# Retention gate applied before the norm's scale, head outputs turned in halves, and one whole-row scatter per expert tile

## The chip, the cores and the metric

The kernel runs on one core of one Trainium2 chip. The metric is device time in microseconds (us) of one execution, lower is better. Engines: PE (TensorE, matmuls and transposes), DVE (VectorE), ACT (ScalarE), POOL (GpSimd) and SP (SyncE, which here only issues DMAs). DMAs issued by SP and ACT go through hardware queues (q1 and q10 in the profile), those issued by POOL through a software queue (q0).

## The reference, cut to what matters

One decoder layer on x of 1024 tokens by 1024 columns, in float32. After a norm and one wide projection, two branches run: sparse attention (8 heads, the top 256 keys of each query) and retention; then a mixture of 16 experts, of which each token uses two. The parts that the change touches:

```python
def group_norm_heads(x, g):                       # x: the retention output of a head, 1024 x 256
    mu = mean(x); var = mean(square(x - mu))
    return (x - mu) * rsqrt(var + EPS) * g
ret = group_norm_heads(retention_chunkwise(...), ret_norm_g)
y_ret = (silu(r_gate) * ret) @ w_ret_branch       # 4 heads of 256 columns

# experts: out[token] += p * expert(token), two experts a token, on top of the residual h
```

## The kernel before, in words

Each engine runs a straight list of instructions, written out by hand; semaphores order the engines. Matmuls are made of three products of a high and a low part (w_hi, w_lo, n_hi, n_lo). Weight chunks of 128x512 come through `w_raw` (SP), are split by ACT (`hi`, line 1512) and POOL (`lo`, line 2644).

**Retention stage.** PE follows `ret_order` (line 646). For head h, `phase1(h)` turns keys and forms scores and chunk states, `phase2(h)` the outputs, `turn(h)` (line 1262) transposes the 8 normed and gated row tiles of `ro` into four banks, named by (j, half). Between them stand four `first_half` products of the attention gates, `first(0)` to `first(3)`. Around this, for a head h: ACT copies the outputs to `ro` (`out_phase2`, line 1697), POOL makes the means (`means`), ACT squares each of the 8 row tiles with the mean as bias (`out_stats`, line 1704), POOL makes 1/sqrt (`scales`, lines 2631 and 2632), DVE scales all tiles by (ro + mean) * rstd and then multiplies by the gate in one 128x2048 instruction (`out_phase2`, lines 2146 and 2149), which sets `o_done`. SP loads the next head's gate after `o_done`, and ACT applies Silu to it (`silu_gate`, line 1668). After PE's turn ACT copies the four banks, with the gains, to `rT_out` and issues the stores to `ret_dram` itself (`out_turn`, lines 1717 and 1720). DVE also copies the gate products to `first_out`, which SP stores (`store_first`). In between DVE searches the top-256 bound of each query row (`pick_top`), a generator of which each call `pick(us)` runs so much; it ends with `dist`, line 2202.

**Start of attention.** STEPS are 64, one for each (query tile t, head h), m = 8t + h. A query tile is loaded by SP to `qrow` (`load_q`), scaled by POOL (`scale_rows`, line 2709), turned by PE in two halves (`turn_q`, line 993; for t >= 2 at steps m = 8(t-1) + 1 and + 4), split by ACT and DVE into `qT_hi` and `qT_lo`. A step is: logits (PE), add of the distances (DVE, 2286), Exp (ACT, 1779), scaling (DVE, 2294), transposes (PE, 1296), copy (ACT, 1800), product with v. `qT_lo(1,1)` and `aT` lie where `rT_out` was, so DVE at (1,1) and ACT at the first `pv` wait for all stores of `ret_dram` (`ret_stored`). POOL issues the copies and accumulating DMAs of weight sums between its query tiles (`copy_sums`, `add_sums`).

**Experts.** 31 tiles of 128 token rows. POOL gathers the rows (`gather_rows`, line 2816), PE does gate, up and down, ACT scales the result by the token's weight into one of three `e_y` buffers (`rows_out`, line 1977), and POOL adds it to the output by indirect DMA (`add_rows`, line 2806): two scatters of half rows (2 KB), each of which waits until the scatter of the same half of the tile before has landed. ACT waits for a buffer's scatters of three tiles before. The end of the kernel waits for all.

Of the kernel before, what the change touches and what calls it, by code (L numbers as in the profile page):

```python
# [198 lines left out]
def program(nc, w, scratch, out):  # L199
    ctx = ExitStack()  # L200
    with ctx:
# [34 lines left out]
        nt_at = place[0]  # L236
        n_hi = sb("n_hi", [P, KT, S], F32R)
# [17 lines left out]
        def r1t(name, shape, off, dt=F32):  # L255
# [26 lines left out]
        rT_out = [r1t(f"rT_out{i}", [P, BANK], at) for i, at in enumerate((18688, 17152, 17664, 18176))]  # L282
        first_out = [sb(f"first_out{i}", [P, BANK], at=at) for i, at in enumerate(
            (up_at, cst_at + 4 * K_TRI, cst_at + 4 * K_REL, cst_at + 4 * (K_REL + BANK)))]
# [17 lines left out]
        qT_lo_first = [r1t(f"qT_lo_first{g}", [P, 4, P], 4096 + 3 * g * S + BANK, F32R) for g in range(2)]  # L302
# [89 lines left out]
        o_mu, o_var, o_rstd, o_done = sem("o_mu"), sem("o_var"), sem("o_rstd"), sem("o_done")  # L392
# [25 lines left out]
        ey_full, ey_read, ey_out = sem("ey_full"), sem("ey_read"), [[sem(f"ey_out{i}{j}") for j in range(2)] for i in range(3)]  # L418
# [233 lines left out]

        SQ_ACT = range(NT - 1)
# [78 lines left out]
        def _(sp):  # L732
# [113 lines left out]
            load_q(1)  # L846
            store_first(3)
# [4 lines left out]
            for i in range(2):  # L852
                sp.wait_ge(first_stored[i], 16 * 8)
# [120 lines left out]
            for i in range(3):  # L974
                for j in range(2):
                    sp.wait_ge(ey_out[i][j], 16 * ((NTILE + 2 - i) // 3))
# [3 lines left out]
        def _(pe):  # L980
# [293 lines left out]
            for m in range(STEPS + LAG + 4):  # L1274
                if m < STEPS:
# [7 lines left out]
                    for k0 in range(0, nk, BANK):  # L1283
                        n = min(BANK, nk - k0)
                        last = three(ps[:, c + k0:c + k0 + n].rearrange("p (t k) -> p t k", k=P),
                                     (qT_hi[t % 2][:, h, :], (qT_lo[t % 2] if t else qT_lo_first)[h // 4][:, h % 4, :]),
# [213 lines left out]
        def _(act):  # L1500
# [200 lines left out]
            def out_stats(h):  # L1701
                act.wait_ge(o_mu, h + 1)
                for c in range(NT):
                    inst = A(junk2[:], ro[h % 2][:, c, :], ACT.Square, bias=small[:, 104 + c:105 + c], accum_out=small[:, 112 + c:113 + c])
                    seq(inst) if c < NT - 1 else inst.then_inc(o_var, 1)
                act.wait_ge(o_var, h + 1)

            def out_turn(h):
                if h == 0:
                    act.wait_ge(proj_last, 64)  # L1710
                for n in range(4):
# [32 lines left out]
            for i in range(4):  # L1744
                c = ga + 4 * i + NH - 1
                if i == 3:
                    out_phase2(3)
                    out_turn(2)
# [10 lines left out]
                if i in (0, 3):  # L1759
                    silu_gate(i)  # L1760
                if i < 3:
                    hi(c + 2)
                    hi(c + 3)
            out_qT(0, 0)
            out_qT(0, 1)
            out_turn(3)
            A(small[:, 497:498], small[:, 500:501], ACT.Exp)

            for m in range(STEPS + LAG + 4):
                if m < STEPS:  # L1770
                    t, h = divmod(m, HA)
                    if m == 7 * HA:
                        for c in range(m6, m6 + NH):
                            hi(c)
                    if m in LATE_AT:
# [5 lines left out]
                if pv_at(m) and pv_at(m)[2] == 3:  # L1781
# [3 lines left out]
                    if t == 0 and g == 0:  # L1785
# [177 lines left out]
            def last_rows_out(i):  # L1963
                n = tile_at(i)
                for j in range(2):
                    act.wait_ge(ey_out[i.buffer][j], 16 * i.third)
# [4 lines left out]
            def rows_out(i):  # L1971
                act.wait_ge(ey_full, i.n + 1)
                if i.reached(3):
                    for j in range(2):
                        act.wait_ge(ey_out[i.buffer][j], 16 * i.third)
# [41 lines left out]
        def _(dve):  # L2017
# [859 lines left out]
```

## Time and profile before

| | |
|---|---|
| three runs | 1491.22, 1497.29, 1498.73 us, median 1497.29 |
| the profiled execution | 1492.21 us, span 1490.1 us, mean granted clock 0.962 |
| busy | PE 1389.7 us (93%), DVE 1115.1, ACT 869.0, POOL 677.2 |
| DMA | 336.76 MB, mean 226 GB/s |

The span runs from the first to the last instruction; about 2.1 us of the execution's time lie outside it. The stages by time in the span: projections until about 485 us, retention until 600, attention 600 to 777, gates, branches and output product until 1150, routing until 1185, experts until the end.

### The profile page before, as it was taken

To read this page: it belongs to the slowest core of one execution; us is meant where nothing else is said; L and a number is where in the kernel's file an instruction comes from. 1 tells how busy PE (TensorE), PEld (TensorE's weight loads), DVE (VectorE), ACT (ScalarE), POOL (GpSimd) and SP (SyncE) were. 2 spreads that over 40 slices of the span, in tenths; PEclk is the share of its full clock that TensorE was granted. 3 is DMA by queue.
4 is the path that set the end of the run, shared out by engine and by line. 5 is a ranking of instruction groups with operands and counts; after the bars stand their busy time and mean duration, and the time that the engine had idled before them with its cause. 6 is when DMAs were issued, how large, how long until landed. Compare 5 with 4: busy or idle time off the path is not lost.

```text
span 1490.1 us, 19630 instructions
## 1 busy us (share of the span) xinstructions
PE 1389.7 (93%) x6518; PEld 1137.7 (76%) x6518; DVE 1115.1 (75%) x1581; ACT 869.0 (58%) x1528; POOL 677.2 (45%) x474
## 2 busy tenths in 40 slices
PE   6999999999999798799999999999997699999995
PEld 6887777788888687667767887887885588888884
DVE  6828999999989954666634447989643699999994
ACT  5237544435773577577744447363345388888884
POOL 3622254445454624121124545555332467665665
PEclk9997999999999999699999999999999699999998
DMA  5997688796765684978958886574346898989995
GB/s 187 360 255 139 161 262 308 205 277 195 259 216 175 207 261 159 258 209 188 250 126 298 225 231 221 197 251 139 111 147 232 300 300 202 311 230 357 282 278 71
DMA packets 153364, 336.76 MB, mean 226 GB/s; under 512 B 14896, under 2 KB 32688, under 8 KB 149040
## 3 DMA queue, kind: packets, MB, share of 16 engines
q1 hardware_dynamic: 111904, 227.49, 44.8%
q0 software_dynamic: 28496, 82.85, 26.1%
q10 hardware_dynamic: 12864, 25.17, 4.5%
q8 instruction: 53, 0.87, 0.2%
q14 instruction: 47, 0.39, 0.1%
HBM read 323.92 MB, written 125.83 MB: 302 GB/s over the span
## 4 chain that ended last, share of the span: by engine, by line
PE 67%; DVE 19%; DMA 4%; ACT 4%; issue 3%; POOL 2%; SPq 0%; ACTq 0%; DVEq 0%; POOLq 0%
PE ps L985 18%; PE ps L987 18%; PE ps L986 18%; DVE hits L2160 4%; PE ps L1306 4%; DVE dist L2123 2%; PE ps L1440 2%; DVE n_lo L2050 2%; PE ps L1296 2%; DMA w_raw<-sums_dram 1%; DMA a_raw<-att_dram 1%; PE ps L1257 1%; DMA ret_dram<-rT_out 1%; DVE ranks L2195 1%; DVE top_change L2177 1%
## 5 line engine op out<-in xcount | busy, mean ns | idle before, releaser
L2644 POOL TENSOR_TENSOR w_lo<-w_raw,w_hi 128x512 fp32r<-128x512 f32 (+1 forms) x264 | 377.4, 1446 | 426.2 <-ACT w_hi L1512 424.0
L1512 ACT CAST w_hi<-w_raw 128x512 fp32r<-128x512 f32 (+1 forms) x264 | 161.0, 617 | 306.4 <-PE ps L987 232.6
L985 PE MATMUL ps<-n_hi,w_hi 128*128 128x512 f32 x624 | 246.0, 394 | 13.6 <-POOL w_lo L2644 9.7
L987 PE MATMUL ps<-n_hi,w_lo 128*128 128x512 f32 x624 | 243.9, 391 | 0.0
L986 PE MATMUL ps<-n_lo,w_hi 128*128 128x512 f32 x624 | 243.8, 391 | 0.0
L2582 DVE TENSOR_TENSOR e_lo<-e_raw,e_hi 128x2048 fp32r<-128x2048 f32 x93 | 213.3, 2295 | 21.9 <-ACT e_hi L1956 21.9
L985 PE MATMUL ps<-w_hi,n_hi 128*128 128x512 f32 (+1 forms) x528 | 204.7, 388 | 8.9 <-POOL w_lo L2644 4.2
L986 PE MATMUL ps<-w_lo,n_hi 128*128 128x512 f32 (+1 forms) x528 | 203.0, 384 | 0.0
L987 PE MATMUL ps<-w_hi,n_lo 128*128 128x512 f32 (+1 forms) x528 | 202.9, 384 | 0.0
L1956 ACT CAST e_hi<-e_raw 128x2048 fp32r<-128x2048 f32 x93 | 177.8, 1914 | 32.5 <-PE ps L987 17.3
L2806 POOL DMA_INDIRECT out<-e_y,dest x62 | 142.9, 2305 | 94.4 <-DMA out<-e_y,dest 66.0
L2160 DVE TENSOR_SCALAR_CACHE_REDUCE hits<-dist,top_bound 128x384 uint8<-128x384 f32 (+2 forms) x192 | 171.9, 940 | 0.4
L985 PEld LDWEIGHTS ps<-n_hi,w_hi 128*128 128x128 f32 x624 | 117.6, 189 | 42.3 <-POOL w_lo L2644 15.7
L987 PEld LDWEIGHTS ps<-n_hi,w_lo 128*128 128x128 f32 x624 | 117.5, 188 | 24.7
L986 PEld LDWEIGHTS ps<-n_lo,w_hi 128*128 128x128 f32 x624 | 117.7, 189 | 24.1 <-issue 0.2
L985 PEld LDWEIGHTS ps<-w_hi,n_hi 128*128 128x128 f32 x528 | 100.9, 191 | 29.6 <-issue 7.1
L987 PEld LDWEIGHTS ps<-w_hi,n_lo 128*128 128x128 f32 x528 | 100.8, 191 | 18.5
L986 PEld LDWEIGHTS ps<-w_lo,n_hi 128*128 128x128 f32 x528 | 101.0, 191 | 17.7
L985 PE MATMUL ps<-e_hi,x_hi 128*128 128x512 f32 x248 | 101.0, 407 | 2.4 <-DVE x_lo L2586 2.4
L987 PE MATMUL ps<-e_hi,x_lo 128*128 128x512 f32 x248 | 97.9, 395 | 0.0
L986 PE MATMUL ps<-e_lo,x_hi 128*128 128x512 f32 x248 | 97.7, 394 | 0.0
L2286 DVE CUSTOM_DVE_ANT_0 prob<-ps,dist 128x128 f32<-128x128 f32 (+7 forms) x64 | 48.4, 756 | 37.9 <-PE ps L987 37.2
(287 smaller groups left out, 2668.3 us busy)
## 6 DMA issues: line engine op xcount, KB each, us to landing
w_raw<-sums_dram SPq DMA_DIRECT2D x128, 256.0 KB, 4.1
e_raw<-in_w_gate SPq DMA_DIRECT2D x64, 512.0 KB
e_raw<-in_w_up SPq DMA_DIRECT2D x64, 512.0 KB
e_raw<-in_w_down SPq DMA_DIRECT2D x32, 1024.0 KB
w_raw<-in_w_in SPq DMA_DIRECT2D x80, 256.0 KB, 4.7
sums_dram<-in_w_in POOLq DMA_DIRECT2D x20, 1024.0 KB, 10.8
sums_dram<-in_w_in SPq DMA_DIRECT2D x16, 1024.0 KB, 11.5
sums_dram<-sums_dram POOLq DMA_DIRECT2D x16, 1024.0 KB, 8.9
```

The lines of the kernel that those rows point to most:

```text
L985: mm(out, a[0], b[0], start=first, stop=False, skip_group_check=skip)
L986: mm(out, a[0], b[1], start=False, stop=False, skip_group_check=skip)
L987: return mm(out, a[1], b[0], start=False, stop=last, skip_group_check=skip)
L1296: last = tr(bank(name)[:, kt % 4 * P:(kt % 4 + 1) * P], prob[h % 4][:, kt * P:(kt + 1) * P], ident)
L1306: last = mm(bank(name), kvu[:, kt, DH:2 * DH], pT[:, kt, g], start=kt == 0, stop=kt == t)
L1512: nc.scalar.copy(w_hi[c % NH][:, :width], split_from(c)[:, :width]).then_inc(hi_ready, 1)
L1956: nc.scalar.copy(split_at(e_hi, i, j)[:], e_raw[i.buffer][j][:]).then_inc(ehi_done[j], 1)
L2160: seq.mark(V.tensor_scalar(hits[i % 2][:, :(t + 1) * P], scores(t), bounds(i), None, op, ALU.add, accum_out=sums[:, i:i + 1]))
L2286: bk.read(V.tensor_tensor_reduce(out=prob[h % 4][:, :nk], in0=ps[:, c:c + nk], in1=dist[:, tile_off(t):tile_off(t) + nk], scale=-(2.0 ** - ...
L2582: V.tensor_tensor(split_at(e_lo, i, j)[:], e_raw[i.buffer][j][:], split_at(e_hi, i, j)[:].bitcast(F32), ALU.subtract).then_inc(elo_done[j], 1)
L2644: G.tensor_tensor(w_lo[c % NH][:, :width], split_from(c)[:, :width], w_hi[c % NH][:, :width].bitcast(F32), ALU.subtract).then_inc(lo_ready, 1)
L2806: G.indirect_dma_start(out=out_halves, out_offset=bass.IndirectOffsetOnAxis(ap=dest[j][:, n:n + 1], axis=0), in_=e_y[i.buffer][:, j * BANK ...
```

## The change

The gate is multiplied in first, by one instruction per row tile, (ro + mean) * gate, each as soon as ACT has squared that tile (`o_sq` in place of `o_var`), and then comes the multiplication by rstd, which counts `o_done` after four and after eight tiles. `o_gated` stands between and is what the next gate's load and the next means wait for. PE's `turn` does the first half of the tiles for both j, then the second. ACT's Silu stands ahead of its squares in all heads. The copies of head 2 go from ACT to DVE and their stores to SP; the Exp table load is moved ahead of `out_qT(0, 0)`. `qT_lo` of the tiles 0 and 1 and `first_out` lie elsewhere, and the waits for `ret_stored` and `first_stored` stand later. The calls of `pick` are spread. The scatter adds whole rows of 4 KB, one per tile.

```diff
-        dest = [sb(f"dest{j}", [P, 32], U32) for j in range(2)]
-        out_halves = out.rearrange("r (j n) -> (r j) n", j=2)
+        dest = sb("dest", [P, 32], U32)
...
+        rT_out.insert(1, sb("rT_out1", [P, BANK], at=up_at))
+        first_out = [sb(f"first_out{i}", [P, BANK], at=n_hi_at + 4 * (i * S + BANK)) for i in range(4)]
...
+        qT_lo_early = [[r1t(f"qT_lo_early{2 * t + g}", [P, 4, P], 4096 + at * S + BANK, F32R) for g, at in enumerate(pair)]
+                       for t, pair in enumerate(((0, 3), (1, 2)))]
...
+        TURN_ORDER = (0, 2, 1, 3)
... sync: load_gate
-                    sp.wait_ge(o_done, h)
+                    sp.wait_ge(o_gated, h)
...
             load_q(1)
+            for n in TURN_ORDER:
+                j, half = divmod(n, 2)
+                bk.wait_read(sp, ("rT", 2, j, half))
+                row = (2 * 2 + j) * P
+                sp.dma_start(ret_dram[row:row + P, half * BANK:(half + 1) * BANK], rT_out[n][:]).then_inc(ret_stored[n % 2], 16)
             store_first(3)
             load_q(2)
...
             sp.wait_ge(dist_done, NT)
-            for i in range(2):
-                sp.wait_ge(first_stored[i], 16 * 8)
             sp.dma_start(cst[:, K_TRI:], w["cst"][:, K_TRI:]).then_inc(rest_in, 16)
... tensor: turn
-                pe.wait_ge(o_done, h + 1)
-                for j in range(2):
-                    for half in range(2):
+                for half in range(2):
+                    pe.wait_ge(o_done, 2 * h + half + 1)
+                    for j in range(2):
... scalar
-                    seq(inst) if c < NT - 1 else inst.then_inc(o_var, 1)
-                act.wait_ge(o_var, h + 1)
+                    inst.then_inc(o_sq, 1)
+                    act.wait_ge(o_sq, NT * h + c + 1)
...
                 if i == 3:
                     out_phase2(3)
-                    out_turn(2)
                 if i in (1, 2):
                     out_phase2(i)
                     out_phase1(i + 1)
                 hi(c)
+                silu_gate(i)
                 out_stats(i)
                 if i in (1, 2):
-                    silu_gate(i)
                     out_turn(i - 1)
                 if i < 3:
                     hi(c + 1)
-                if i in (0, 3):
-                    silu_gate(i)
...
+            A(small[:, 497:498], small[:, 500:501], ACT.Exp)
             out_qT(0, 0)
             out_qT(0, 1)
             out_turn(3)
-            A(small[:, 497:498], small[:, 500:501], ACT.Exp)
...
-                    if t == 0 and g == 0:
+                    if t == 1 and g == 0:
                         for i in range(2):
                             act.wait_ge(ret_stored[i], 32 * HR)
... vector
             def out_phase2(h):
-                dve.wait_ge(o_rstd, h + 1)
-                for c in range(NT):
-                    inst = V.tensor_scalar(ro[h % 2][:, c, :], ro[h % 2][:, c, :], small[:, 104 + c:105 + c], small[:, 120 + c:121 + c], ALU.add, ALU.mult)
-                seq(inst)
-                dve.wait_ge(silu_done, h + 1)
-                V.tensor_tensor(ro[h % 2][:], ro[h % 2][:], gate[:], ALU.mult).then_inc(o_done, 1)
+                dve.wait_ge(silu_done, h + 1)
+                for c in range(NT):
+                    dve.wait_ge(o_sq, NT * h + c + 1)
+                    inst = V.scalar_tensor_tensor(ro[h % 2][:, c, :], ro[h % 2][:, c, :], small[:, 104 + c:105 + c], gate[:, c, :], ALU.add, ALU.mult)
+                inst.then_inc(o_gated, 1)
+                dve.wait_ge(o_gated, h + 1)
+                dve.wait_ge(o_rstd, h + 1)
+                for c in range(NT):
+                    inst = V.tensor_scalar(ro[h % 2][:, c, :], ro[h % 2][:, c, :], small[:, 120 + c:121 + c], None, ALU.mult)
+                    if c % 4 == 3:
+                        inst.then_inc(o_done, 1)
+
+            def out_turn(h):
+                for n in TURN_ORDER:
+                    j, half = divmod(n, 2)
+                    name = ("rT", h, j, half)
+                    dve.wait_ge(ret_stored[n % 2], 32 * h)
+                    bk.wait_full(dve, name)
+                    bk.read(V.tensor_scalar(rT_out[n][:], bank(name), gains[:, GRT + 2 * h + j:GRT + 2 * h + j + 1], None, ALU.mult), name)
...
             pick(8)
             out_phase1(1)
-            pick(1e9)
+            pick(3)
             out_phase2(0)
             keep_first(0)
+            pick(3)
...
-                if (t, g) == (2, 0):
-                    dve.wait_ge(first_stored[0], 16 * 8)
-                if (t, g) == (1, 1):
+                if (t, g) in ((2, 0), (3, 1)):
                     for i in range(2):
                         dve.wait_ge(ret_stored[i], 32 * HR)
...
                 out_phase2(i)
                 keep_first(i)
+                pick(1e9)
+            out_turn(2)
             out_phase2(3)
...
-            for j in range(2):
-                inst = V.tensor_scalar(dest[j][:], row_at, 2.0, float(j), ALU.mult, ALU.add)
-            inst.then_inc(dest_done, 1)
+            V.tensor_copy(dest[:], row_at).then_inc(dest_done, 1)
... gpsimd
-                for j in range(2):
-                    pool.wait_ge(ey_read, i.n + 1 + (j if (i + 1).reached(NTILE) else 0))
-                    if i.reached(1):
-                        pool.wait_ge(ey_out[(i - 1).buffer][j], 16 * ((i - 1).third + 1))
-                    G.indirect_dma_start(out=out_halves, out_offset=bass.IndirectOffsetOnAxis(ap=dest[j][:, n:n + 1], axis=0),
-                                         in_=e_y[i.buffer][:, j * BANK:(j + 1) * BANK], in_offset=None,
-                                         compute_op=ALU.add).then_inc(ey_out[i.buffer][j], 16)
+                pool.wait_ge(ey_read, i.n + 1 + ((i + 1).reached(NTILE)))
+                if i.reached(1):
+                    pool.wait_ge(ey_out[(i - 1).buffer], 16 * ((i - 1).third + 1))
+                G.indirect_dma_start(out=out, out_offset=bass.IndirectOffsetOnAxis(ap=dest[:, n:n + 1], axis=0),
+                                     in_=e_y[i.buffer][:], in_offset=None,
+                                     compute_op=ALU.add).then_inc(ey_out[i.buffer], 16)
```

## Rows read from the trace of the kernel before

**Rows 1.** Windows: us, each engine's busy time (instructions), clock, DMA share, GB/s.
```profile
580.00:600.00 20.00, 13.65 (x67) 11.65 (x65) 10.18 (x15) 11.14 (x27) 7.73 (x8) 0.84 0.49 159
1300.00:1400.00 100.00, 100.00 (x495) 84.52 (x494) 92.95 (x65) 86.78 (x76) 61.26 (x31) 1.00 0.96 294
```
**Rows 2.** Timeline of 505 to 530: start, us, engine, line [idle before <- releaser].
```profile
511.09 1.23 DVE L2202 SCALAR_TENSOR_TENSOR dist<-cst,dist 128x1024 f32<-128x1024 f32 x1
...
512.35 1.23 DVE L2131 TENSOR_TENSOR sT<-sT,cst 128x1024 f32<-128x1024 f32 x1
...
518.16 2.07 PE L1257 MATMUL ps<-rv,sT 128*128 128x256 f32 x4 [5.87 <-DVE state L2137]
```
**Rows 3.** Timeline, the last head from ACT's copies of head 2 to the first Exp.
```profile
577.62 0.68 ACT L1717 ACTIVATE rT_out<-ps,gains 128x512 f32<-128x512 f32 x1
...
582.19 0.62 ACT L1512 CAST w_hi<-w_raw 128x512 fp32r<-128x512 f32 x1 [0.45 <-ACT rT_out L1717]
...
587.79 2.19 ACT L1668 ACTIVATE gate<-gate 128x512 f32<-128x512 f32 x4
...
588.12 1.63 POOL L2632 TENSOR_TENSOR small<-small 128x8 f32<-128x8 f32 x1
...
589.79 4.41 DVE L2146 TENSOR_SCALAR ro<-ro,small 128x256 f32<-128x256 f32 x8 [17.06 <-POOL small L2632]
589.83 1.90 POOL L2709 TENSOR_TENSOR qrow<-qrow,small 128x1024 f32<-128x1024 f32 x1
...
591.67 2.78 POOL L2685 DMA_DIRECT2D sums_dram<-in_w_in  x4
...
596.58 3.68 PE L1269 MATMUL ps<-cst,ro 128*128 128x128 f32 x16 [6.35 <-DVE ro L2149]
...
602.31 1.28 ACT L1767 ACT_TABLE_LOAD   x1 [0.39 <-ACT rT_out L1717]
...
603.71 0.39 ACT L1779 ACTIVATE prob<-prob,small 128x128 f32<-128x128 f32 x1
```
**Rows 4.** Timeline of 586 to 632, what the first steps of attention wait for.
```profile
600.94 0.60 SPq L799 DMA_DIRECT2D qrow<-proj_dram  x1
...
613.91 0.69 DVE L2266 TENSOR_TENSOR qT_lo<-ps,qT_hi 128x512 fp32r<-128x512 f32 x1 [2.45 <-DMA ret_dram<-rT_out]
...
614.83 1.89 POOL L2709 TENSOR_TENSOR qrow<-qrow,small 128x1024 f32<-128x1024 f32 x1 [20.38 <-DMA qrow<-proj_dram]
...
617.12 1.06 PE L993 MATMUL ps<-cst,qrow 128*128 128x128 f32 x4
```
**Rows 5.** DMA queues of 600 to 602: packets, MB, share; then an issue and its landing time.
```profile
q0 software_dynamic: 105, 0.41, 90.2%
...
qrow<-proj_dram SPq DMA_DIRECT2D x1, 512.0 KB, 13.8
```
**Rows 6.** DMA queues of 604 to 606.
```profile
q0 software_dynamic: 104, 0.37, 51.8%
q10 hardware_dynamic: 102, 0.20, 27.4%
```
**Rows 7.** The chain of waits in the experts: start, us, what.
```profile
1358.45 0.90 PE ps L1440 x8
1367.81 0.90 PE ps L1440 x8
```
**Rows 8.** All issues: KB each, median us to landing; then the scatter line's own.
```profile
e_x<-n_dram,token POOLq DMA_INDIRECT x31, 9.5
```
**Rows 9.** The scatters of line 2806, 62 of them, from issue to landing.
```profile
DMA to landing us min/median/max: 4.6/7.3/12.1
```
**Rows 10.** The chain of waits at the end: start, us, what.
```profile
1474.26 4.69 DMA out<-e_y,dest
```
**Rows 11.** POOL's timeline at the end: the first half of tile 29, the last of tile 30.
```profile
1471.11 1.55 POOL L2806 DMA_INDIRECT out<-e_y,dest  x1 [1.06 <-ACT e_y L1977]
...
1479.70 1.55 POOL L2806 DMA_INDIRECT out<-e_y,dest  x1 [1.59 <-DMA out<-e_y,dest]
```

More of the change, by code:

```diff
@@ L236, in program @@
         nt_at = place[0]
+        n_hi_at = place[0]
         n_hi = sb("n_hi", [P, KT, S], F32R)
@@ L281, in program @@
         gate = r1t("gate", [P, NT, DV], 15104)
-        rT_out = [r1t(f"rT_out{i}", [P, BANK], at) for i, at in enumerate((18688, 17152, 17664, 18176))]
-        first_out = [sb(f"first_out{i}", [P, BANK], at=at) for i, at in enumerate(
-            (up_at, cst_at + 4 * K_TRI, cst_at + 4 * K_REL, cst_at + 4 * (K_REL + BANK)))]
+        rT_out = [r1t(f"rT_out{i}", [P, BANK], at) for i, at in ((0, 18688), (2, 17664), (3, 18176))]
+        rT_out.insert(1, sb("rT_out1", [P, BANK], at=up_at))
+        first_out = [sb(f"first_out{i}", [P, BANK], at=n_hi_at + 4 * (i * S + BANK)) for i in range(4)]
         junk2 = r1t("junk2", [P, DV], 7168)
@@ L301, in program, with qT_lo_of @@
              (wr_at + 4 * BANK * (NR + 2 * NH - 1), r1 + 4 * 18432)])]
-        qT_lo_first = [r1t(f"qT_lo_first{g}", [P, 4, P], 4096 + 3 * g * S + BANK, F32R) for g in range(2)]
+        qT_lo_early = [[r1t(f"qT_lo_early{2 * t + g}", [P, 4, P], 4096 + at * S + BANK, F32R) for g, at in enumerate(pair)]
+                       for t, pair in enumerate(((0, 3), (1, 2)))]
+        def qT_lo_of(t, g):
+            return qT_lo_early[t][g] if t < 2 else qT_lo[t % 2][g]
         prob = [r1t(f"prob{i}", [P, S], 4096 + i * S) for i in range(4)]
@@ L417, in program @@
         slot_done = sem("slot_done")
-        ey_full, ey_read, ey_out = sem("ey_full"), sem("ey_read"), [[sem(f"ey_out{i}{j}") for j in range(2)] for i in range(3)]
+        ey_full, ey_read, ey_out = sem("ey_full"), sem("ey_read"), [sem(f"ey_out{i}") for i in range(3)]
         dest_done, p_done2 = sem("dest_done"), sem("p_done2")
@@ L1710, in out_turn @@
                     act.wait_ge(proj_last, 64)
-                for n in range(4):
+                for n in TURN_ORDER:
                     j, half = divmod(n, 2)
@@ L1774, in _ @@
                             hi(c)
+                    if m == LATE_AT[0]:
+                        for i in range(2):
+                            act.wait_ge(first_stored[i], 16 * 8)
                     if m in LATE_AT:
@@ L1964, in last_rows_out @@
                 n = tile_at(i)
+                act.wait_ge(ey_out[i.buffer], 16 * i.third)
                 for j in range(2):
-                    act.wait_ge(ey_out[i.buffer][j], 16 * i.third)
                     act.wait_ge(ey_full, i.n + 1 + j)
@@ L1973, in rows_out @@
                 if i.reached(3):
-                    for j in range(2):
-                        act.wait_ge(ey_out[i.buffer][j], 16 * i.third)
+                    act.wait_ge(ey_out[i.buffer], 16 * i.third)
                 n = tile_at(i)
@@ L2143, in out_phase2 @@
             def out_phase2(h):
+                dve.wait_ge(silu_done, h + 1)
[4 more added lines that the diff above has]
+                dve.wait_ge(o_gated, h + 1)
                 dve.wait_ge(o_rstd, h + 1)
                 for c in range(NT):
[L2146 to L2149 removed]
+                    inst = V.tensor_scalar(ro[h % 2][:, c, :], ro[h % 2][:, c, :], small[:, 120 + c:121 + c], None, ALU.mult)
+                    if c % 4 == 3:
+                        inst.then_inc(o_done, 1)
+            def out_turn(h):
+                for n in TURN_ORDER:
+                    j, half = divmod(n, 2)
[3 more added lines that the diff above has]
+                    bk.read(V.tensor_scalar(rT_out[n][:], bank(name), gains[:, GRT + 2 * h + j:GRT + 2 * h + j + 1], None, ALU.mult), name)
             def scores(t):
@@ L2265, in out_qT @@
                 name = ("qT", t, g)
-                bk.read(V.tensor_tensor((qT_lo[t % 2] if t else qT_lo_first)[g][:].rearrange("p h q -> p (h q)"), bank(name),
+                bk.read(V.tensor_tensor(qT_lo_of(t, g)[:].rearrange("p h q -> p (h q)"), bank(name),
                                         qT_hi[t % 2][:, 4 * g:4 * g + 4, :].rearrange("p h q -> p (h q)").bitcast(F32), ALU.subtract), name)
@@ L2568, in _ @@
             seq(V.scalar_tensor_tensor(row_at, row_at, -1.0, tok_at, ALU.add, ALU.add))
-            for j in range(2):
-                inst = V.tensor_scalar(dest[j][:], row_at, 2.0, float(j), ALU.mult, ALU.add)
-            inst.then_inc(dest_done, 1)
+            V.tensor_copy(dest[:], row_at).then_inc(dest_done, 1)
             def slot_weights():
@@ L2715, in means @@
                 if h:
-                    pool.wait_ge(o_done, h)
+                    pool.wait_ge(o_gated, h)
                 G.tensor_scalar(small[:, 104:112], small[:, 96:104], -1.0 / DV, 0.0, ALU.mult, ALU.add).then_inc(o_mu, 1)
             def scales(h):
-                pool.wait_ge(o_var, h + 1)
+                if h:
+                    pool.wait_ge(o_done, 2 * h)
+                pool.wait_ge(o_sq, NT * (h + 1))
                 rstd(small[:, 120:128], small[:, 112:120], NT, DV, (o_rstd, 1))
@@ L2831, in _ @@
             for i in range(3):
-                for j in range(2):
-                    pool.wait_ge(ey_out[i][j], 16 * ((NTILE + 2 - i) // 3))
+                pool.wait_ge(ey_out[i], 16 * ((NTILE + 2 - i) // 3))
             for j in range(3):
```

8 lines of the change are left out of this document (3 added, 5 removed).

## The prediction

> **What bounds the kernel now.** I read the windows first. PE is the engine of most of the time: in the experts it is busy for 100.00 of 100 us at full clock, DMA at 0.96 beside it, and a tile starts every 1367.81 - 1358.45 = 9.36 us [rows 1, 7]. Nothing that the change does to DVE, ACT or POOL there can pay, except at the very end. At the end of retention it is otherwise: from 580 to 600 PE is busy for 13.65 us of 20 and its clock falls to 0.84 [rows 1]. So the timeline was read from there on. PE stands idle twice in retention: 5.87 us before 518.16, for DVE's states of head 1 [rows 2], and 6.35 us before 596.58, for the gated tiles of head 3 [rows 3]. Then comes a chain that PE only follows: turn of head 3, four copies by ACT, table load, first Exp at 603.71 [rows 3], and in attention's first tiles waits for DMAs: DVE 2.45 us for the last stores of `ret_dram`, POOL 20.38 us for `qrow(2)`, which is scaled just in time for PE's turn at 617.12 [rows 4].
>
> **The pick calls: nothing.** The last instruction of the search (L2202, 511.09) already stands before the states of head 1 (L2131, 512.35) [rows 2]: `pick(8)` ends the search, and `pick(1e9)` behind it finds nothing to do. So the first stall of 5.87 us stays. Here the change does not do what it says. Had it moved work, at most those 5.87 us could be won, which is outside my sum.
>
> **Heads 0 to 2: nothing.** DVE has 8 + 8 small instructions in place of 8 + one large one. The large one ends a semaphore before PE's turn at 596.58, so it takes 596.5 - (589.79 + 4.41) = 2.3 us. Eight small ones cost 2.5 (the 4.41 of a scaling less the 1.90 of POOL's instruction beside it) [rows 3]. PE turns head h only after the outputs of head h + 1, and the next gate is loaded sooner, so all of it is covered. If it were not, it would cost 0.2 us a head and a semaphore, 1 in all.
>
> **Head 3, up to the scale.** ACT loses its four copies of head 2: from 577.62 to 582.19, 4.57 us [rows 3], of which DVE now has 4 copies in a time when it waits (17.06 us idle) [rows 3], and SP four stores, issued before the gate products of `store_first(3)`, which are not there before DVE makes them. In their place Silu, 2.19 us, comes ahead of the squares; the cast of 0.62 was there before too. The squares start at 577.62 + 0.62 + 2.19 = 580.4 and take 587.79 - 582.81 = 5.0, so they end at 585.5 in place of 587.79. That is 2.2 us. POOL's 1/sqrt follows (0.3 + 1.63), and DVE starts to scale at 587.6 in place of 589.79.
>
> **Head 3, behind the scale.** Before: 4.41 + 2.3 and a semaphore, so PE's turn began 6.8 us after the scale began [rows 3]. After: four tiles. They still collide with POOL's 1.90 us multiplication of `qrow(1)`, which stands right behind 1/sqrt in both kernels, so 1.9 + 4 x 0.31 = 3.1 us: first half ready at 590.7, second at 592.0. The other instruction, (ro + mean) * gate, follows each square and is done but for the last tile (0.4 us) when the scale arrives. PE ends its last `first_half` at 590.2 (idle 6.35 before 596.58), so what is late next on PE is PE itself. ACT's copies begin at about 591.3 (before: 602.31 - 0.39 - 4.1 = 597.8). They end at about 595.4; the table load of 1.28 us and its 0.1 of issue lie in ACT's idle time ahead of them. If the load were needed twice, for Exp and for the copies' function, that costs 2.6. First Exp at about 595.9 in place of 603.71: 7.8 us gained at this point.
>
> The Trainium skill has a rule for the collision (page "SBUF — State Buffer", section Who interferes with whom): DVE and GpSimd share a port pair as an exclusive lock, so whichever comes second waits for the whole instruction. The 4.41 us for eight tiles beside POOL's 1.90 us agree. By the rule alone the 1.9 us would stay in the changed kernel, as in my sum; without a collision the first half would be ready 1.9 earlier, but PE would be no earlier than 590.2.
>
> **What is late next.** The wait for the stores of `ret_dram` (2.45 us) goes, since the (1,1) buffer lies elsewhere; at (2,0) the stores have had until about 612 to land. But PE's step 9 needs `qrow(2)`. Its load is issued behind `store_first(3)`: DVE makes those after its `out_qT`, two of 0.69 [rows 4]. The load was issued 4.4 us after DVE's end at 596.5, so now at 592.0 + 4.4 = 596.4 in place of 600.94 [rows 4]. It took 13.8 us to land [rows 5], because POOL's four copies of 1 MB, issued at 591.67 [rows 3], hold the DMA engines: from 600 to 602 q0 alone moved data, at 90.2% of the engines [rows 5], though SP and ACT had issued before; from 604 to 606 q0 has 51.8% and ACT's queue alone 27.4% [rows 6]. POOL issues the copies at 589.6 now, 2.1 earlier. Lower bound: `qrow(2)` keeps its own 13.8: landed at 596.4 + 13.8 = 610.2. Upper: the burst ends as long after the copies as before (600.94 + 13.8 - 591.67 = 23.1): 612.7. The constants' load (364 KB, now not behind the wait for `first_stored`) adds at most 364/512 of a `qrow`, under 1 us, to the same queue, behind `qrow(2)`. I take 611.0, nearer its own time, since stores and load move together as they did before. POOL scales in 1.9 and PE turns 0.3 later, at 613.2 in place of 617.12: 3.9. Meanwhile ACT and DVE have finished steps 8 and 9, which at 617.12 they had not (DVE was put back by 2.45); I put that at 1.3 between 0 and 2.5. **Attention: 5.2 us gained, bounds 2.2 and 7.8** (landed at 612.7 and nothing advanced, and the whole of the head start). Later `qrow` tiles and POOL's accumulating DMAs are issued off PE's and POOL's progress, so they move with it, and the stages behind are PE-bound.
>
> A rule of the Trainium skill speaks to this point (page "DMA: Bandwidth & Descriptors", Queues, rings and completion order, on arbitration): each engine goes round the queue rows that have work, packet by packet. The first two microseconds do not show that (q0 alone); from 604 on the shares come near it. What it would make of the time is rival 2.
>
> **The scatter.** POOL issues 31 in place of 62, and per tile saves one of some 2.3 us, hidden by PE in both kernels. At the end: before, the half scatter issued at 1474.26 landed 4.69 later [rows 10], and the last was issued at 1479.70 [rows 11] and lands by 1484.3; what follows until 1490.1 I leave as it is. After: tile 29's scatter is issued when its first half was, at 1471.1 [rows 11]; tile 30's rows are ready before it has landed, so it waits for it. A whole row is not in the trace. From below it is a half's 4.6 [rows 9], from above a half's end after a second one's issue, 1.55 + 4.69 = 6.2 [rows 10, 11]; gathers of whole rows took 9.5 in the loaded stage where halves took 7.3 [rows 8, 9], a ratio of 1.3, so 5.9. Landing of 29 at 1477.0, issue of 30 at 1477.7 (0.75 from landing to issue, as 1479.70 - 1474.26 - 4.69), landing at 1483.6. **0.7 us gained, bounds +3.3 (4.6 twice) and -1.6 (landing times of 7).** One DVE instruction less for `dest` is off the path.
>
> **Sum.** 1492.2 (the profiled execution: span 1490.1 and 2.1 around it) - 5.2 - 0.7 = 1486.3. That execution was the second lowest of four: with the three runs the middle is 1494.8, and the runs spread over 7.5 us. 1494.8 - 5.9 = 1488.9 is what I give as the time; against the median of 1497.29 about 3 more may be spread.
>
> **Rivals.**
> 1. The burst decides alone: `qrow(2)` lands at 612.7 or later, the advance of ACT and DVE is lost in PE's clock, which stands at half after the longer wait. Gain 2.2 + 0.7: 1491.9. For it: q0 alone in the first microseconds [rows 5]. Against: `qrow(2)` is issued 4.6 earlier. Chance 0.19.
> 2. The hardware queues get their turn at once, or `qrow(2)` is in early: all of 7.8 stays, 8.5 with the tail: 1486.3. For it: the shares from 604 on [rows 6]. Against: 600 to 602 [rows 5]. Chance 0.26.
> 3. Slower: whole-row scatters fall behind PE. Scatter i+1 is issued only when i has landed, so a tile costs its landing plus 0.75. With halves that is 7.3 + 0.75 = 8.05 under 9.36 [rows 7, 9]. With whole rows at the end's difference (5.9 - 4.6) it is 8.6 + 0.75 = 9.35, just PE's pace, and at the gather's 9.5 it is 10.25, 0.9 a tile over PE. Three `e_y` buffers hide 2 x 9.36 = 18.7 us of lag, but the end waits for the lag: 27 tiles x 0.9 = 24, less 8 that the last three tiles win back when the weights are in (9.36 - 6.65 each). So 16 against attention's 5.2: 1494.8 - 5.2 + 16 = 1505.6. It decides from a landing of 8.9 us on. For it: DMA share 0.96 [rows 1], half scatters up to 12.1 [rows 9]. Against: the bytes are the same with half the packets. Chance 0.14.
> 4. The pipeline absorbs the head start by other waits of attention (POOL's chain of accumulating DMAs): 0.7 only: 1494.1. Chance 0.03.
>
> The forecast has 0.38. Likeliest one's own range: 1483 to 1494. The range for 8 in 10 takes in rivals 1, 2 and the spread of the runs, and the mild half of rival 3: 1480 to 1500.
>
> A measurement tells 0.5%, about 7.5 us, from no change. The forecast's 5.9 is under it, with a third of its chance beyond it through the unknown landings: 0.12 faster, 0.26 same. Rival 2 at 8.5: 0.22 faster, 0.04 same. Rivals 1 and 4: same, 0.22. Rival 3: slower but for its mild cases, 0.12, and 0.02 same. Faster 0.34, same 0.54, slower 0.12.
>
> **What the changed profile would show.** PE without the 6.35 before the turn of head 3 and with it at about 590 to 592; the first Exp at about 596; no wait of DVE for `ret_dram`; POOL's scaling of `qrow(2)` at about 611 and PE's turn at 613; the idle of 5.87 before 518 unchanged; tiles of the experts still 9.36 apart; whole-row scatters landing in 8 to 9 us, uncontended in 5.9. I am wrong if the scatters' median is over 8.9, if the table load comes twice, or if PE's turn of step 9 comes outside 610 to 616.

## The result, and the profile after

The changed kernel takes 1512.52 us (1509.13 to 1515.12 over three runs) against 1497.29: a ratio of 1.0086 with a 95% interval from 1.0051 to 1.0121, so it is slower by 0.86%, some 13 us. The forecast was 1488.9, its range 1480 to 1500. The profiled execution took 1509.13, its span is 1506.7.

Both halves of the change show in the trace. First the head start of attention: the timeline of the changed kernel, from POOL's 1/sqrt of the last head to the third query tile, to be set beside [rows 3, 4].

```profile
589.33 1.63 POOL L2649 TENSOR_TENSOR small<-small 128x8 f32<-128x8 f32 x1
591.04 1.90 POOL L2726 TENSOR_TENSOR qrow<-qrow,small 128x1024 f32<-128x1024 f32 x1
591.07 4.19 DVE L2157 TENSOR_SCALAR ro<-ro,small 128x256 f32<-128x256 f32 x8 [1.88 <-POOL small L2649]
592.88 2.63 POOL L2702 DMA_DIRECT2D sums_dram<-in_w_in  x4
594.03 0.66 PE L1276 MATMUL ps<-cst,ro 128*128 128x128 f32 x4 [0.38 <-DVE ro L2157]
...
599.51 0.57 SPq L804 DMA_DIRECT2D qrow<-proj_dram  x1
...
600.05 0.40 ACT L1785 ACTIVATE prob<-prob,small 128x128 f32<-128x128 f32 x1 [0.40 <-ACT rT_out L1724]
...
616.25 1.89 POOL L2726 TENSOR_TENSOR qrow<-qrow,small 128x1024 f32<-128x1024 f32 x1 [20.74 <-DMA qrow<-proj_dram]
...
618.20 1.11 PE L1000 MATMUL ps<-cst,qrow 128*128 128x128 f32 x4 [7.79 <-POOL qrow L2726]
```

PE's idle time of 6.35 us ahead of the turn has shrunk to 0.38, and the first Exp is 3.66 us earlier than in [rows 3] although this execution was 2.46 us late before the edit does anything (L2136's product, the one of 512.35 in [rows 2], starts at 514.81). That is 6.1 us. Then PE waits 7.79 us for `qrow(2)`, and its turn, at 617.12 in [rows 4], is at 618.20. The DMA view of 600 to 602 has the load's issue and its time to land, 13.8 in [rows 5]:

```profile
q0 software_dynamic: 106, 0.39, 58.7%
q10 hardware_dynamic: 105, 0.20, 27.3%
q1 hardware_dynamic: 51, 0.10, 14.4%
...
qrow<-proj_dram SPq DMA_DIRECT2D x1, 512.0 KB, 16.7
```

Three queues share the engines there, where q0 was alone in [rows 5], and still the load takes longer. The Trainium skill (page "DMA: Bandwidth & Descriptors", Queues, rings and completion order) has each engine go round the rows with work packet by packet; this trace is nearer to that than the one before, and it did not bring the load in early, as rival 2 would have it.

Next the experts. The view of the instructions that touch `e_y` in the changed kernel: the scatters, what they wait for, who waits for them, and their landing ([rows 9]).

```profile
L2824 POOL DMA_INDIRECT out<-e_y,dest x31: 1552/1690/3634, 1206.0 to 1494.9; - x31
...
  DMA out<-e_y,dest: 162.5, 29
...
  ACT e_y L1982: 8.5, 3
...
DMA to landing us min/median/max: 5.9/7.9/13.2
```

From the first issue to the last a tile takes (1494.9 - 1206.0) / 30 = 9.63 us, over the 9.36 of [rows 7]. The median landing of 7.9 doesn't explain this; the chain that ended last does, since there the landings stand one after another (start, us, what):

```profile
1389.13 11.85 DMA out<-e_y,dest
1401.02 0.75 issue
1401.77 7.84 DMA out<-e_y,dest
1409.65 0.75 issue
1410.40 10.90 DMA out<-e_y,dest
1421.34 0.75 issue
1422.09 11.01 DMA out<-e_y,dest
1433.14 0.75 issue
1433.90 10.49 DMA out<-e_y,dest
...
1473.62 6.77 DMA out<-e_y,dest
1480.43 0.71 issue
1481.14 6.15 DMA out<-e_y,dest
1487.33 0.71 issue
1488.04 6.11 DMA out<-e_y,dest
```

Four of the first five take 10.5 to 11.9 us, over PE's pace; the last three, when all weights are loaded, take 6.1 to 6.8. The lag passes through the three `e_y` buffers to ACT, and then to PE, which is busy for 100 of 100 us from 1300 to 1400 as in [rows 1] and has its gaps behind 1400 (the windows, columns as there):

```profile
1400.00:1440.00 40.00, 37.21 (x179) 30.38 (x178) 33.80 (x25) 32.30 (x29) 14.79 (x8) 1.00 0.97 329
1440.00:1480.00 40.00, 38.81 (x178) 32.10 (x178) 33.34 (x23) 30.23 (x28) 11.01 (x6) 0.96 0.60 126
1480.00:1506.70 26.70, 3.02 (x12) 2.17 (x12) 0.42 (x1) 1.45 (x3) 4.66 (x3) 0.67 0.39 59
```

On ACT, whose timeline follows, the scaled rows of a tile wait for their buffer three times:

```profile
1421.38 1.12 ACT L1982 ACTIVATE e_y<-ps,small 128x1024 f32<-128x1024 f32 x1 [1.39 <-DMA out<-e_y,dest]
1433.19 1.12 ACT L1982 ACTIVATE e_y<-ps,small 128x1024 f32<-128x1024 f32 x1 [3.83 <-DMA out<-e_y,dest]
1444.47 1.11 ACT L1982 ACTIVATE e_y<-ps,small 128x1024 f32<-128x1024 f32 x1 [3.31 <-DMA out<-e_y,dest]
...
1483.65 0.69 ACT L1974 ACTIVATE e_y<-ps,small 128x512 f32<-128x512 f32 x1 [0.61 <-PE ps L994]
```

The account of the two traces: the last scatter is issued at 1494.90, 15.2 us behind the 1479.70 of [rows 11]. The first rows are gathered at 1173.91 instead of 1170.16, which is 3.75 of it. ACT's last `e_y` starts at 1483.65 where it started at 1474.58, so another 5.3 was lost between, where the waits of ACT shown above (8.5 us in all) stand. The rest, 6.15, is the queue of scatters at the end: from that last `e_y` to the last issue 11.25 us pass in place of 5.1.

### The profile page after: what moved, and what is told of

The parts are those of the page before. It is cut to its first block, busy times and chain, and to the rows that moved or that the text cites. A ratio compares the mean times of both kernels' runs of the same rounds, so it can differ in the third digit from the quotient of the medians.

```text
span 1506.7 us, 19601 instructions
## 1 busy us (share of the span) xinstructions
PE 1391.5 (92%) x6518; PEld 1134.5 (75%) x6518; DVE 1119.1 (74%) x1612; ACT 865.3 (57%) x1524; POOL 597.1 (40%) x443
## 4 chain that ended last, share of the span: by engine, by line
PE 48%; DVE 23%; DMA 15%; issue 5%; ACT 5%; POOL 3%; SPq 1%; ACTq 0%; DVEq 0%; POOLq 0%
PE ps L992 13%; PE ps L994 12%; PE ps L993 12%; DVE hits L2178 7%; DMA out<-e_y,dest 7%; PE ps L1313 4%; DVE n_lo L2055 2%; DVE dist L2128 2%; PE ps L1303 2%; DMA sums_dram<-in_w_in 2%; DMA t_raw<-turned_dram 2%; PE ps L1447 1%; POOL w_lo L2661 1%; DMA qrow<-proj_dram 1%; DVE top_change L2195 1%
## 5 line engine op out<-in xcount | busy, mean ns | idle before, releaser
L992 PE MATMUL ps<-n_hi,w_hi 128*128 128x512 f32 x624 | 246.6, 395 | 12.3 <-POOL w_lo L2661 10.4
L992 PEld LDWEIGHTS ps<-n_hi,w_hi 128*128 128x128 f32 x624 | 117.9, 189 | 41.4 <-POOL w_lo L2661 14.6
L2824 POOL DMA_INDIRECT out<-e_y,dest x31 | 64.3, 2073 | 183.1 <-DMA out<-e_y,dest 153.9
```

Source lines behind the costliest of these rows:

```text
L992: mm(out, a[0], b[0], start=first, stop=False, skip_group_check=skip)
L2824: G.indirect_dma_start(out=out, out_offset=bass.IndirectOffsetOnAxis(ap=dest[:, n:n + 1], axis=0), in_=e_y[i.buffer][:], in_offset=None, c ...
```

## Experiments

All kernels here were timed against the kernel before in five rounds, in three groups, each group with the kernel before on one and the same chip; its medians there are 1498.2, 1498.8 and 1498.3. Ratios are to it, and kernels of different groups are compared by their ratios.

**Taking the change apart.** The first kernel has the scatter part of the diff alone, the second the retention part alone.

> The kernel before with the scatter of whole rows alone; nothing of the retention heads is changed. Theory A (the whole-row scatters are the loss: each waits for the landing of the one before it, and one landing with its issue lasts longer than the two half rows' landings lasted side by side): the last scatter is issued about 11 us later than in the kernel before, and the time is 9 to 12 us longer, about 1507. Theory B (the retention edit is the loss, and what the experts lose is carried over from it): within 2 us of the kernel before. Under A the PE is below 95% busy from the start of the last fifteen tiles on, and the scatters' median gap is over 9.4 us.

> The changed kernel with the two scatters of half rows back; the retention edit is all that is left of the change. Theory A (the whole rows are the loss): the time is that of the kernel before within 4 us, on either side; what the trace of the changed kernel shows ahead of the experts (3.7 us later from the first to the last store of attention) is partly run to run. Theory B (the retention edit is the loss): 8 us or more longer. My recorded forecast for this part by itself was 5.2 us shorter; the load of the third query tile landing 16.7 us after its issue instead of 13.8 should bring that to 1 to 2 us shorter.

Whole rows alone: 1509.94, ratio 1.0076 [1.0054, 1.0098]. Retention edit alone: 1496.24, ratio 0.9986 [0.9972, 1.0000], about 2 us gained. So the loss is the scatter's, 11 to 12 us, and theory B falls. In the trace with whole rows alone the last scatter is issued at 1494.2, 14.5 us behind the 1479.70 of [rows 11], of which 4.0 had passed before the first gather (1174.17). Two signs set for theory A did not come: PE is 96% busy from 1343 to 1482, not below 95%, and the median step from one scatter's issue to the next is 8.8 us, not over 9.4. It is the mean that is over PE's pace, (1494.2 - 1206.4) / 30 = 9.59 us; why the two differ is told below.

**What in the whole rows costs.** The third kernel keeps them, but lets them overlap; the fourth keeps the halves and adds a dependency.

```diff
-                if i.reached(1):
-                    pool.wait_ge(ey_out[(i - 1).buffer], 16 * ((i - 1).third + 1))
-                G.indirect_dma_start(out=out, ...
+                if i.reached(2):
+                    pool.wait_ge(ey_out[(i - 2).buffer], 16 * ((i - 2).third + 1))
+                G.indirect_dma_start(out=scratch["spare"] if i.n % 2 else out, ...
```

> As the kernel before with whole-row scatters, but the scatters of odd tiles add their rows to a scratch tensor instead of the output (so half of the experts' contribution is left out of the output), and each scatter waits for the landing of the one two tiles before it. Bytes, rows and instructions are the same. If the chain of landings is what costs (theory A), the loss is gone: within 2 us of the kernel before or 1 to 5 us shorter, and PE over 97% busy in the experts. If whole rows cost by their bytes in the queue or by the time that GpSimd spends on issuing them, the time stays at that of the whole rows alone, 9 to 12 us longer than before.

```diff
                     if i.reached(1):
-                        pool.wait_ge(ey_out[(i - 1).buffer][j], 16 * ((i - 1).third + 1))
+                        for k in range(2):
+                            pool.wait_ge(ey_out[(i - 1).buffer][k], 16 * ((i - 1).third + 1))
```

> The kernel before, two scatters of half rows to a tile, but each of them waits for the landing of both halves of the tile before. The same bytes and descriptors as before, one more dependency. If the loss comes from one chain that includes the last byte of a tile (theory A), part of it shows here: 3 to 10 us longer than the kernel before. If it comes from the whole row's own landing (rows of 4 KB against 2 KB), the kernel is within 2 us of before.

Two destinations: 1497.86, ratio 0.9989 [0.9972, 1.0007]. The loss is gone, with the same rows, bytes and instructions. This kernel changes two things at once, the destination and the wait, but it was not that the landings got shorter: those to `out` have a median of 10.2 us, those to the scratch tensor 7.1, all together 10.1 where whole rows alone have 7.5. Halves that wait for both halves: 1542.48, ratio 1.0291 [1.0266, 1.0316], 44 us and far over the 3 to 10 expected. There the first half of a tile waits for the second of the last one, which is issued later than the first, so a tile costs that delay, a landing and the next issue: (1537.0 - 1212.0) / 30 = 10.8 us from the first scatter to the last. ACT waited 42.7 us for `e_y` in that trace. It is the chain that costs, and two chains side by side are what the two halves were good for.

**Why the chain is too slow.** A pair of kernels without the traffic of the weights:

```diff
-                G.tensor_scalar(fresh[:, 1:31], small[:, 465:495], 0.0, 1.0, ALU.max, ALU.min)
+                G.tensor_scalar(fresh[:, 1:31], small[:, 465:495], 0.0, 0.0, ALU.max, ALU.min)
```

> The kernel before with whole-row scatters, and the loads of the experts' weights are switched off from the fourth tile on (all tiles after the third compute with weights that are there already, so the experts' contribution is not the reference's). Theory A2 (a whole row's landing fits the pace of a tile, 9.36 us, when it has the queues for itself, 5.8 us and 0.7 to the next issue, and exceeds it only beside a new expert's 3 MB of weights, 10 to 12.3 us): the loss of 12 us against the same with half rows shrinks to 0 to 3 us, landings have a median under 6.5 us and PE keeps its pace to the last tile. Rival (the whole row in one chain is slower in itself): it stays over 8 us slower than the half rows with the same loads switched off.

> The kernel before, half-row scatters, with the loads of the experts' weights switched off from the fourth tile on, as the pair of the kernel above. All theories: within 2 us of the kernel before, since PE is at its pace of 9.36 us a tile there already; the median landing of the half rows falls from 7.3 us to about 5.

Whole rows: 1498.96, ratio 1.0007 [0.9986, 1.0027]. Halves: 1498.45, ratio 0.9999 [0.9981, 1.0017]. The loss of whole rows is gone here as well. Their line in the `e_y` view with the loads switched off:

```profile
L2800 POOL DMA_INDIRECT out<-e_y,dest x31: 1552/2496/2797, 1204.6 to 1481.0; - x31
...
  ACT e_y L1974: 119.4, 29
  DMA out<-e_y,dest: 10.4, 2
...
DMA to landing us min/median/max: 5.9/7.1/7.8
```

The scatters wait for ACT, that is for PE, 29 times, and twice for a landing; in the changed kernel 29 waits ended with a landing, 26 of scatters and 3 of ACT. The median landing (7.1, where under 6.5 was expected) is hardly lower than the 7.5 with the weights' traffic: what went is the part above 7.8. The halves' median without that traffic is 5.9, where about 5 was expected. The DMA views of the kernel with whole rows alone show the neighbour. From 1345 to 1356, beside the weights on q1 and one gather, a scatter took 12.3 us; from 1460 to 1466 another, with nothing beside it, took 5.8:

```profile
q1 hardware_dynamic: 742, 3.31, 73.9%
q0 software_dynamic: 205, 0.74, 28.8%
...
out<-e_y,dest POOLq DMA_INDIRECT x1, 12.3
```

```profile
q0 software_dynamic: 144, 0.52, 53.3%
...
out<-e_y,dest POOLq DMA_INDIRECT x1, 5.8
```

**Where retention's gain went.** On the kernel with the retention edit alone, first POOL's four copies are issued behind the scaling of `qrow(2)`; then SP's load is also issued ahead of the last head's stores; then only the latter.

```diff
-            copy_sums((4,))
             for t in range(2, NT):
                 scale_rows(t)
-                if t < 5:
-                    add_sums(t - 2, (4,))
-                elif t == 5:
+                if t == 2:
+                    copy_sums((4,))
+                elif t < 6:
+                    add_sums(t - 3, (4,))
+                if t == 5:
                     copy_sums((5,))
-                elif t == 6:
-                    add_sums(0, (5,))
-                    add_sums(1, (5,))
+                elif t > 5:
+                    add_sums(t - 6, (5,))
```

```diff
-            store_first(3)
             load_q(2)
+            store_first(3)
```

> The retention edit alone (two half-row scatters to a tile, as before), and GpSimd issues the four copies of 1 MB to sums_dram behind the scale of the third query tile in place of ahead of it; what follows on that chain moves with them. Theory C (the start of attention is eaten by the copies: the load of the third query tile, issued at 598.7, shares the queues with 4 MB of copies and lands only about 16 us later): the load lands within 8 us, the PE's wait ahead of step 9 shrinks from 7.8 us to under 1, and the time is 3 to 7 us shorter than with the retention edit alone, 1489 to 1493 on the scale where the kernel before is at 1498. Rival D (attention is bound by something later, as the copies of the next group or the softmax, so that an early third tile is given back by the last store): within 1.5 us of the retention edit alone.

> As the one before it, and SyncE issues the load of the third query tile ahead of the four stores of the last retention head to n_dram (1 MB) in place of behind them. Theory C: another 0 to 1.5 us shorter, since the stores are the other large transfer beside that load. Rival D: no difference from the kernel with the copies moved alone, within 1 us.

> The retention edit alone, with one line of SyncE moved: the load of the third query tile is issued ahead of the last head's four stores instead of behind them, and the copies stay where they were. In the kernel with both moves that load was issued at 586.2 instead of 598.7, ahead of the copies at 592.8. Theory C (the copies cost the start of attention only because the third tile's load is issued after them): 7 to 12 us shorter than the retention edit alone, the same as with the copies moved, about 1487. Rival (the copies delay the fourth tile and the later ones as well): 3 to 6 us shorter only.

Copies moved: 1486.54, ratio 0.9923 [0.9892, 0.9953]. Both moved: 1488.54, 0.9932 [0.9912, 0.9953]. Load alone: 1489.70, 0.9942 [0.9923, 0.9961]. The timeline with the copies moved:

```profile
597.28 1.20 SPq L805 DMA_DIRECT2D qrow<-proj_dram  x1
...
603.59 1.90 POOL L2731 TENSOR_TENSOR qrow<-qrow,small 128x1024 f32<-128x1024 f32 x1 [12.54 <-DMA qrow<-proj_dram]
605.43 2.61 POOL L2707 DMA_DIRECT2D sums_dram<-in_w_in  x4
```

The tile is scaled 6.3 us after its load was issued, where with the edit alone it was 17.3 (598.72 to 616.07), and PE has no wait for it. The gain on top of the edit, 9.4 us by the ratios (9.7 by the medians, which are of two chips), is larger than the 3 to 7 expected. Theory C holds, rival D falls. Both moves together give no more than the copies alone, where up to 1.5 us more was expected, so they remove the same wait. The load alone gives 6.6 us by the ratios, a little under the 7 to 12 of theory C; what it costs is seen below.

The last three ask whose gain it is: the kernel before with the copies moved, the changed kernel with the copies moved, the kernel before with the load moved (same diffs).

> The kernel before, nothing of the change in it, with GpSimd's copies issued behind the scale of the third query tile. It tells how much of the 12 us of the kernel with both belongs to the retention edit. Theory C (the edit's head start is real and was only hidden by the wait for the third tile): 5 to 8 us shorter than the kernel before, 1490 to 1493, and the retention edit on top of it is worth 4 to 6 us. Rival E (the retention edit gives nothing even then, its place on the path was taken by the copies all along): 11 to 13 us shorter, as with the edit.

> The changed kernel (whole-row scatters and the retention edit) with the copies issued behind the scale of the third query tile. If the two effects are apart from each other: the changed kernel's time less the 9.7 us that the moved copies gave with the retention edit alone, 1499 to 1502, so about the time of the kernel before. If the experts take up an earlier start (more slack, fewer loads at the time), 1495 or less.

> The kernel before, nothing of the change in it, with SyncE's load of the third query tile ahead of the last head's stores. Theory C: as the kernel before with the copies moved, 5 to 8 us shorter than before, if in the old order of the heads the tile's buffer and its first users are ready before the copies are issued at 591.7; if the load can't be issued ahead of them it stays within 2 us of before.

They took, in this order, 1493.76, ratio 0.9980 [0.9963, 0.9997]; 1500.17, ratio 1.0011 [0.9997, 1.0025]; and 1497.85, ratio 0.9997 [0.9980, 1.0014]. Copies moved without the edit give 3 us and not 5 to 8, nor the 11 to 13 of rival E. The edit without the copies moved gives 2, both together 11.5; so the edit is worth 8.5 on top of the moved copies, where 4 to 6 was expected. The changed kernel with the copies moved is in its range of 1499 to 1502. Each waits for the other: with the edit alone `qrow(2)` is late, with the copies moved alone head 3 is. The load moved in the old order of the heads was issued ahead of the copies, which is the case for which theory C had 5 to 8 us, and it still gave nothing: counted from the mark of the table below, the first store came 0.9 us earlier, but the first Exp 4.2 us later. The trace of this kernel shows what held the Exp back:

```profile
594.85 7.62 DVE L2146 TENSOR_SCALAR ro<-ro,small 128x256 f32<-128x256 f32 x8 [17.09 <-POOL small L2632]
...
594.89 1.90 POOL L2709 TENSOR_TENSOR qrow<-qrow,small 128x1024 f32<-128x1024 f32 x1
...
599.43 1.91 POOL L2709 TENSOR_TENSOR qrow<-qrow,small 128x1024 f32<-128x1024 f32 x1
```

DVE's scaling of head 3 takes 7.62 us where it took 4.41 in [rows 3]. That is 3.2 of the 4.2; the rest is that it began 0.95 us later. Beside it POOL now scales two query tiles, with the issue of its four copies between them, since the third tile has landed early; in [rows 3] it scales one. The load moved on top of the retention edit shows the same, 7.33 us where the edit alone has 4.18, and its first Exp is 3.6 us later. So an early load has a price on DVE here, which the moved copies do not have (3.86 us). That the second scaling by POOL is the cause is read from these traces; no run takes it away by itself.

| kernel | ratio | search to first store of attention | gather to end |
|---|---|---|---|
| before | 1 | 117.2 | 319.9 |
| changed | 1.0086 | 114.6 | 332.8 |
| whole rows alone | 1.0076 | 117.5 | 331.7 |
| retention alone | 0.9986 | 114.4 | 318.9 |
| before, copies moved | 0.9980 | 114.2 | 322.3 |
| before, load moved | 0.9997 | 116.3 | 320.2 |
| retention, copies moved | 0.9923 | 106.1 | 322.6 |
| retention, load moved | 0.9942 | 110.3 | 320.6 |
| retention, both moved | 0.9932 | 107.6 | 322.6 |
| changed, copies moved | 1.0011 | 106.2 | 335.4 |

The third column is from the start of `sT`'s product (512.35 in [rows 2]) to the first store to `att_dram`, the fourth from the first gather of `e_x` to the end of the span, each from one trace. They separate what the time of one execution mixes. The last column also shows something that no run here explains: wherever the copies are moved it is 2.0 to 3.7 us longer than in the same kernel without that, so some of what they gain at the start of attention is lost again behind the first gather.

## Why the prediction was wrong

The step that failed is the scatter's term. The likeliest case put a whole row's landing in the loaded stage at 8.6 us and so a tile at 9.35, equal to PE's pace: the stage cost nothing, and a gain of 0.7 us was left at the end, bounds +3.3 and -1.6. It was a loss of some 12 us (11.4 by the ratio of whole rows alone, 11.8 to 13.9 by the last column of the table, from pairs of kernels that differ in the scatter alone or before against changed). The terms:

- **Pick calls: right.** The idle time before 518 is 5.88 us (5.87 in [rows 2]).
- **Head 3: right in mechanism, short by 1.7 us.** First Exp 6.1 us earlier by the account above, forecast 7.8. PE, which I had as what is late next, waits 1.23 us for DVE's `out_qT` between the first and the second half of its turn, and the scale began 1.2 us earlier and not 2.2: the squares ended 1.5 earlier, and POOL's first instruction behind them took 0.42 us where it had taken 0.20. The table load came once, at 588.69, in ACT's idle time.
- **`qrow(2)`: rival 1.** I had it land 14.6 us after its issue (596.4 to 611.0); it took 16.7 from 599.51. The turn of step 9, for which I had set 610 to 616 as the range, came at 618.20; less the 2.46 us by which this execution was late it is 615.7, at the end of the range. Attention's gain was 2.6 us to the first store, near the lower bound of 2.2, not 5.2. The end of the burst decided, as in the upper case: the load landed 23.3 us after the copies were issued at 592.88, and that case had 23.1.
- **The uncontended landing: about right.** 6.15 and 6.11 us near the end and 5.9, the shortest, for the last one; forecast 5.9. (4.6 times 9.5/7.3, which it was worked out from, is 6.0.)
- **The contended landing: wrong.** I took 8.6, the halves' median of 7.3 and the difference at the end, 5.9 - 4.6, on top of it. With whole rows alone, the 30 steps from one scatter's issue to the next fall into two groups: 16 of 6.4 to 9.2 us and 14 of 10.6 to 13.1. In a chain what counts is their sum. In the changed kernel five steps, from the issue at 1389.13 to that at 1445.18, take 56.1 us, 11.2 a tile, 1.9 over PE. The row that warned of it was the maximum of 12.1 in [rows 9], and I had used it only as an argument for rival 3.

Rival 3 is what happened: its mechanism, its place, and nearly its size. I priced it at 16 us and 1505.6, of which some 12 came, and gave it 0.14. It had one landing of 9.5 us for every tile, though, and not landings in two groups. Its threshold was wrongly put: "decides from a landing of 8.9 on" and "wrong if the median is over 8.9" read the median, which was 7.9 while the stage fell behind. The bounds of the sum (+3.3, -1.6) covered only the tail; the contended landing had no upper bound in the sum, although the gather's 9.5 [rows 8] stood beside it.

What lies ahead of the experts in the two traces, 3.75 us later at the first gather, need not be the change's. The kernels that are the same as before up to there had their first gather at 1171.98, 1174.17, 1174.44, 1177.85 and 1179.75, and the product of [rows 2] between 511.48 and 516.11. From the first to the last store of attention they took 149.9 to 152.4 us, the changed kernel 152.1 and the kernel before, in its one trace, 148.4.

The version to keep is the retention edit with two half-row scatters and the copies behind the third query tile: 0.9923 of the kernel before, where the changed kernel has 1.0086.

## What to carry to other kernels

Before merging two transfers that wait for their own predecessors, count the chains: two chains of halves may overlap where one of wholes can't, and halving the instructions is worth nothing if the engine that issues them has time. Judge a chain by the sum of its landings over the busiest stretch, never by a median, and against the pace of the engine that feeds it. When a stage starts earlier, look at which loads its first steps wait for and what large transfers are issued just ahead of them; the head start is worth only what those loads allow, and each of two such limits tested alone looks small (2 and 3 us here, 11.5 together).

## What the runs showed of the hardware

- A scatter with add of 128 rows of 4 KB landed in 5.7 to 6.8 us at the end of the kernel, when no weights are loaded any more, and in 10 to 13 us beside an expert's weights (in one window q1 had 74% of the engines' time and q0 29%). With the weights' loads switched off the median was 7.1 us and the longest 7.8.
- A load of 512 KB issued 6.6 us behind four copies of 1 MB on GpSimd's queue took 16.7 us to be landed. Without them it was in use 6.3 us after its issue.
- Eight DVE scalings of 128x256 took 3.9 to 4.4 us beside one GpSimd instruction of 1.90 us, 5.8 us beside two of them in a row, and 7.3 and 7.6 us beside two with the issue of four copies between them.
- The same program ahead of a point reached it at times up to 9.6 us apart (the first gather, 1170.16 to 1179.75), so one trace beside another can't price an edit of a few us; a difference taken inside each trace, from a mark just ahead of the edit, repeated within 0.9 us (116.8 to 117.7 in six traces).
